# A two-layer hybrid trunk: shifted rows by DMA during the projections, with token shift, convolution and silus computed there

## The chip, the cores and the metric

The kernel runs on one core of one Trainium2 chip. The time is device microseconds of one execution; the number compared is the median of the runs. Engines are named as in the profile: PE (TensorE; PEld is its weight loads), DVE (VectorE), ACT (ScalarE), POOL (GpSimd) and SP (SyncE). Each has its own instruction queue and runs it in order; semaphores order them against each other. DMAs are issued by SP, ACT and POOL.

## The reference

384 tokens (128 context, 256 latent) of width 1024 pass two layers, all in float32. Each layer is a modulated norm, an input projection, a pair of mixers, an output projection, and a mixture of 64 experts. Two steps between projection and mixers mix neighbouring tokens of one sequence. In layer 0 a token shift, on the last 1792 of 2560 columns:

```python
def centred_token_shift(x, mu):
    xp = jnp.pad(x, ((0, 0), (1, 1), (0, 0)))
    neighbours = 0.5 * (xp[:, :-2] + xp[:, 2:])
    return x + mu * (neighbours - x)
```

In layer 1 a convolution over three neighbouring tokens with a weight per column and tap, followed by a silu, on 1536 of 3600 columns; and a silu of 512 further columns (z) that multiplies the delta mixer's normed output at its end:

```python
cqkv = jax.nn.silu(centred_depthwise_conv(cqkv, p['c_conv']))
oc = rms_norm(oc, p['c_onorm']) * jax.nn.silu(heads(cz))
```

The context tokens and the latent tokens are separate sequences, so the rows before the first and after the last token of each count as zero.

## The kernel before

Tokens lie on partitions, 128 to a tile: tile 0 is the context, tiles 1 and 2 the latents. The projection's result `proj` is in SBUF as [128 partitions, 3 tiles, columns]. A neighbouring token is thus on the next partition; between tiles 1 and 2 it is on the far end of another tile.

The work is written out by hand as one program per engine, in phases. `end_phase` makes PE, ACT and DVE wait for each other. In the projection (a loop over column blocks `EVEN_BLOCKS` or `ODD_BLOCKS`, and in each over three tiles; k counts the tiles) PE multiplies into six PSUM banks in turn; DVE copies even k to SBUF, ACT odd k, and PE waits before tile k for the copy of tile k - 6 (the semaphores `proj_saved`). Beside its copies DVE makes the sums for the query and key norms after k = 6 (`head_sums`) and the norms and rotations after k = 8, 10 and 12 (`head_norm`). Weights come into a ring of six slots by SP, which waits only for free slots.

After layer 0's projection `token_shift` (PE L616, DVE L1607) works in four blocks of 448 columns: PE multiplies each tile by a shift matrix of ones beside the diagonal, with an extra matmul for the edge between tiles 1 and 2, and DVE makes three operations per tile. Meanwhile ACT issues `load_cached` (L1214), the loads of cached keys, values, states and small weights: eight DMAs in layer 0, three in layer 1. A second `end_phase` closes the step.

After layer 1's projection `convolution` (PE L631, DVE L1618) works in three blocks of 512 columns: PE makes two shifted copies in six banks, DVE five operations per tile, and PE waits for DVE before the next block. Then ACT (`conv_silu`, L1231) makes exp(-x) of each tile's 1536 columns and DVE adds one, takes the reciprocal and multiplies. `load_cached` comes after the phase's end.

`attend` starts with PE's transposes of queries and keys. ACT first issues two output stores, then copies the transposed queries; the first scores wait for these copies and for the cached keys and values (`parts_loaded`). In `delta`'s last lines ACT makes exp(-z) behind a reciprocal root, and DVE, which waits for both, scales the output, makes the sigmoid of z (`sigmoid_of`, L1504), multiplies it by z and then into `mixed`, for which the output projection waits.

POOL clears corners of the mixers' matrices, loads parameters after each layer's mixers, and runs the experts' gathers and scatters. Most helpers have one line for all their calls: PE's `mm` L544, DVE's tensor_tensor L1485, scalar_tensor_tensor L1493, copy L1499 and reciprocal L1502, ACT's activation L1139.

## Time and profile before

| | |
|---|---|
| median of three runs | 2902.38 us (2894.6 to 2909.49) |
| the profiled execution | 2891.6 us, span 2889.9 us |
| PE busy | 2235.4 us, 77% of the span |
| DVE busy | 871.9 us, 30% |
| ACT busy | 337.0 us, 12% |
| POOL busy | 178.5 us, 6% |
| layer 0's projection (58.5 to 166.6 us) | 108.1 us, PE busy 106.84 |
| token shift, to attention's first transpose | 166.6 to 195.5 us |
| layer 1's projection (1549.7 to 1710.8 us) | 161.1 us, PE busy 158.63 |
| convolution, then silus, to attention's first transpose | 1710.8 to 1767.6 to 1807.0 us |
| silu of z at the delta mixer's end | 2099.8 to 2112.3 us |

Busy shares are averages over stages with different limits; what one stage costs is read from its own stretch and from what ends the waits there. A timeline row gives the start, the duration (of all instructions that it merges), the engine, the line, the operation, its output and inputs, the shapes, the count, and in brackets the engine's idle time before it with what ended it. ACTq, SPq and POOLq are those engines' DMA issues. A row of the table of stretches gives the stretch and its length, the busy time and instructions of PE, PEld, DVE, ACT and POOL, the mean granted clock of PE as a share of 2.4 GHz, the DMA engines' busy share and GB/s.

### The profile page before, as it was taken

The page shows a single profiled execution, that of the slowest core. Times are in us where ns is not written, and L with a number is a line of the kernel's source. Part 1 is how long each engine was busy: PE and PEld are TensorE (multiplying, and loading weights), DVE is VectorE, ACT ScalarE, POOL GpSimd, SP SyncE. Part 2 cuts the span into 40 slices and gives each one's busy share as a digit, 9 for nine tenths or more (in the row PEclk, how much of TensorE's full clock was granted, in tenths as well). Part 3 has the DMA queues.
Part 4 walks back from the last instruction along what each step waited for, and adds up shares of the span by engine and source line. Part 5 has one row for each costly group of instructions (what it writes and reads, how often), then busy time and mean ns, then how long its engine had stood idle before and what let it go on. Part 6 is the DMA issues. An engine that isn't in the chain of part 4 may idle for free.

```text
span 2889.9 us, 37837 instructions
## 1 busy us (share of the span) xinstructions
PE 2235.4 (77%) x16075; PEld 1520.3 (53%) x16075; DVE 871.9 (30%) x1512; ACT 337.0 (12%) x747; POOL 178.5 (6%) x200
## 2 busy tenths in 40 slices
PE   5978887777778888898937981957667788889882
PEld 1445666666645555555513440657665555555551
DVE  1243333333452111111132317265636211111114
ACT  0013111111011111111100000300000111111110
POOL 0000000000001111111100000000000111111110
PEclk9985878877888999999978986568888999999996
DMA  7220323311325999999980220000002799999995
GB/s 282 102 77 15 126 97 119 118 60 60 48 110 215 384 377 381 386 372 372 369 346 29 88 88 0 22 1 3 7 19 97 261 390 391 381 382 382 371 381 197
DMA packets 120703, 571.19 MB, mean 198 GB/s; under 512 B 24944, under 2 KB 28272, under 8 KB 69072
## 3 DMA queue, kind: packets, MB, share of 16 engines
q1 hardware_dynamic: 85392, 496.07, 44.2%
q0 software_dynamic: 28448, 60.42, 6.2%
q10 hardware_dynamic: 6688, 12.18, 1.2%
q8 instruction: 133, 2.18, 0.3%
q14 instruction: 42, 0.34, 0.0%
HBM read 566.42 MB, written 48.30 MB: 213 GB/s over the span
## 4 chain that ended last, share of the span: by engine, by line
PE 61%; DMA 17%; DVE 15%; issue 3%; ACT 1%; SPq 1%; PEldq 0%; PEld 0%; POOL 0%; DVEq 0%; ACTq 0%; POOLq 0%
PE bank L544 56%; DMA ring<-in_exp_w_up 11%; DVE arena L1485 9%; DMA ring<-in_exp_w_down 3%; DMA ring<-in_mod_w 2%; DVE arena L1502 1%; PE bank L1047 1%; PE bank L676 1%; DVE arena L1493 1%; PE bank L1071 1%; DVE mixed L1485 1%; DMA arena<-choice_rows 1%; DVE arena L1499 1%; DVE hT L1490 1%; ACT arena L1139 1%
## 5 line engine op out<-in xcount | busy, mean ns | idle before, releaser
L544 PE MATMUL bank<-ring,arena 128*64 128x256 f32 (+3 forms) x5168 | 928.9, 443 | 137.7 <-DMA ring<-in_exp_w_up 85.8
L544 PEld LDWEIGHTS bank<-ring,arena 128*64 128x64 f32 (+1 forms) x5168 | 570.5, 157 | 463.8 <-issue 357.0
L544 PE MATMUL bank<-arena 64*64 64x64 f32 (+8 forms) x6176 | 426.1, 255 | 54.7 <-DVE arena L1485 41.8
L544 PEld LDWEIGHTS bank<-arena 64*64 64x64 f32 (+5 forms) x6176 | 367.6, 161 | 89.4 <-DVE arena L1485 41.5
L1499 DVE COPY arena<-bank 128x512 f32<-128x512 f32 (+4 forms) x231 | 151.7, 663 | 624.8 <-PE bank L544 560.4
L544 PE MATMUL bank<-ring,hT 128*128 128x512 f32 (+2 forms) x672 | 265.5, 555 | 21.9 <-DVE hT L1490 18.9
L1493 DVE SCALAR_TENSOR_TENSOR arena<-bank,arena 128x256 f32<-128x256 f32 (+2 forms) x96 | 47.5, 494 | 682.3 <-PE bank L544 681.6
L544 PEld LDWEIGHTS bank<-ring,hT 128*128 128x128 f32 x672 | 128.4, 200 | 159.0 <-issue 136.5
L1485 DVE TENSOR_TENSOR arena<-arena 128x512 f32<-128x512 f32 (+9 forms) x175 | 155.1, 909 | 53.8 <-DMA arena<-choice_rows 42.7
L544 PE MATMUL bank<-arena,consts 64*64 64x64 f32 (+5 forms) x516 | 114.7, 417 | 64.2 <-DVEq L1630 20.6
L2173 POOL DMA_INDIRECT arena<-token_rows,arena x80 | 80.6, 1008 | 933.2 <-PE bank L1047 642.7
L544 PE MATMUL bank<-hT,ring 128*128 128x384 f32 x384 | 125.6, 488 | 4.0 <-DVE arena L1485 2.3
L544 PEld LDWEIGHTS bank<-arena,consts 64*64 64x64 f32 (+2 forms) x516 | 59.9, 208 | 109.5 <-issue 62.8
L544 PEld LDWEIGHTS bank<-hT,ring 128*128 128x128 f32 x384 | 104.8, 274 | 23.0 <-DVE arena L1485 3.6
L1047 PE MATMUL bank<-consts,arena 128*128 128x128 f32 x640 | 100.1, 280 | 15.7 <-DMA arena<-token_rows,arena 15.7
L2179 POOL DMA_INDIRECT choice_rows<-arena x80 | 79.7, 996 | 345.0 <-DVE arena L1499 341.1
L1485 DVE TENSOR_TENSOR arena<-bank,consts 128x256 f32<-128x256 f32 (+1 forms) x156 | 74.4, 501 | 84.7 <-PE bank L544 84.7
L1047 PEld LDWEIGHTS bank<-consts,arena 128*128 128x128 f32 x640 | 75.7, 144 | 38.3 <-issue 35.0
L1485 DVE TENSOR_TENSOR arena<-arena,bank 128x512 f32<-128x512 f32 (+3 forms) x150 | 82.5, 563 | 32.9 <-PE bank L544 31.8
L544 PE MATMUL bank<-ring,cond 128*2 128x256 f32 x768 | 61.0, 466 | 32.0 <-DMA ring<-in_mod_w 32.0
L1139 ACT ACTIVATE arena<-bank 128x256 f32<-128x256 f32 (+3 forms) x104 | 42.7, 423 | 352.2 <-PE bank L544 352.2
L1429 ACT COPY arena<-bank 128x256 f32<-128x256 f32 x80 | 29.8, 372 | 451.3 <-PE bank L1071 451.3
(166 smaller groups left out, 1190.8 us busy)
## 6 DMA issues: line engine op xcount, KB each, us to landing
ring<-in_exp_w_gate SPq DMA_DIRECT2D x128, 1024.0 KB, 10.4
ring<-in_exp_w_up SPq DMA_DIRECT2D x128, 1024.0 KB, 10.1
ring<-in_exp_w_down SPq DMA_DIRECT2D x128, 1024.0 KB, 10.3
ring<-in_mod_w SPq DMA_DIRECT2D x48, 1024.0 KB, 9.2
arena<-choice_rows POOLq DMA_DIRECT2D x6, 3072.0 KB, 11.3
ring<-in_od_w_in SPq DMA_DIRECT2D x14, 1024.0 KB, 8.6
ring<-in_ev_w_in SPq DMA_DIRECT2D x10, 1024.0 KB, 15.3
ring<-in_ev_w_out SPq DMA_DIRECT2D x4, 1024.0 KB, 8.8
```

What stands on the lines that cost most here:

```text
L544: return nc.tensor.matmul(out, lhsT, rhs, start=start, stop=stop, **kw)
L676: last = nc.tensor.transpose(bank[2 + u % 2][:, k * P:(k + 1) * P], A.p[:, u % 2, k * P:(k + 1) * P], C["ident"])
L1047: last = nc.tensor.transpose(bank[half][:, c * P:(c + 1) * P], g_x[x.b][:, (4 * half + c) * P:(4 * half + c + 1) * P], C["ident"])
L1071: last = nc.tensor.transpose(bank[4][:, c * P:(c + 1) * P], g_h[x.b][:, c::2], C["ident"])
L1139: return nc.scalar.activation(out, in_, func, **kw)
L1429: nc.scalar.copy(g_ht[x.b], heads(bank[4][:, 0:2 * P], 2)).then_inc(sem("ht_saved"), 1)
L1485: return nc.vector.tensor_tensor(out, a, b, op)
L1490: return nc.vector.tensor_scalar(out, a, s1, s2, op0, op1)
L1493: return nc.vector.scalar_tensor_tensor(out=out, in0=a, scalar=s, in1=b, op0=op0, op1=op1)
L1499: return nc.vector.tensor_copy(out, a)
L2173: nc.gpsimd.indirect_dma_start(g_x[x.b], None, x_rows[l], row(x, 0), bounds_check=NTOK - 1, oob_is_err=False).then_inc(sem("expert_loaded" ...
L2179: nc.gpsimd.indirect_dma_start(y_rows[l], row(x, 1), g_y[x.b], None, bounds_check=TOP_K * NTOK - 1, oob_is_err=False).then_inc(sem("scatte ...
```

## The change

The shift matrices, the shift and convolution steps on PE, and the separate silu steps are gone. While a projection runs, ACT issues for each finished block of shifted columns (four in layer 0, three in layer 1, each of up to 512 columns by three tiles) six SBUF-to-SBUF DMAs that write the block displaced by one partition down (`back`) and up (`ahead`): each displaced copy is made of a block of 112 and one of 15 partitions, and two single rows bridge tiles 1 and 2. POOL clears the edge partitions beforehand. DVE computes shift and convolution from the block and its two displaced copies, two or three tiles later, for all three tiles at once. In layer 1 ACT makes the sigmoids, of the convolved blocks and of z, by exp, ln and exp, and DVE multiplies. Layer 0's last block is loaded and shifted after the last tile. The sigmoids' scratch is `mixed`; the displaced copies lie in the part of the arena that attention uses later, so `load_cached` comes after the phase's end in both layers. The second `end_phase` stays.

The layout, and the steps taken out of PE's order:

```diff
+        near_at = [[(po0, po0 + 1536), (17000, 18536)], [(po1, po1 + 1536), (po1 + 3072, 18700)]]
+        SHIFTED = [EVEN_BLOCKS[2:], ODD_BLOCKS[2:5]]
+        SHIFT_DONE = [3 * (2 + i) + 2 for i in range(4)]
...
-                (token_shift if l % 2 == 0 else convolution)()
```

ACT:

```diff
+            def saved(eng, l, k):
+                eng.wait_ge(sem("proj_saved", 0), 9 * l + k // 2 + 1)
+                eng.wait_ge(sem("proj_saved", 1), 9 * l + (k + 1) // 2)
+
+            def load_near(l, i):
+
+                (a, b), n = SHIFTED[l][i], len(SHIFTED[0]) * l + i
+                saved(act, l, SHIFT_DONE[i])
+                act.wait_ge(sem("near_cleared"), l + 1)
+                if i >= 2:
+                    act.wait_ge(sem("near_used"), n - 1)
+                x = proj_of(l)[0][:, :, a:b]
+                back, ahead = (buf[:, :, 0:b - a] for buf in near[l][i % 2])
+                s = sem("near_loaded", i % 2)
+                for p, q in ((0, P - 16), (P - 16, P - 1)):
+                    load(back[p + 1:q + 1, :, :], x[p:q, :, :], s)
+                    load(ahead[p:q, :, :], x[p + 1:q + 1, :, :], s)
+                load(back[0:1, 2, :], x[P - 1:P, 1, :], s)
+                load(ahead[P - 1:P, 1, :], x[0:1, 2, :], s)
+
+            def sigmoid_block(i):
+
+                if i < 3:
+                    act.wait_ge(sem("near_used"), len(SHIFTED[0]) + i + 1)
+                else:
+                    saved(act, 1, SHIFT_DONE[3])
+                if i >= 2:
+                    act.wait_ge(sem("silu_done"), i - 1)
+                e = wide_scratch[i % 2].rearrange("p (t n) -> p t n", t=TILES)
+                link(f(e, proj1[:, :, 512 * i:512 * (i + 1)], ACT.Exp, scale=-1.0))
+                link(f(e, e, ACT.Ln, bias=one_col))
+                f(e, e, ACT.Exp, scale=-1.0).then_inc(sem("sigmoid_ready"), 1)
...
                     for t in range(TILES):
+                        if l and k in (12, 15, 18, 20):
+                            sigmoid_block((12, 15, 18, 20).index(k))
+                        for i in range(len(SHIFTED[l])):
+                            if k == SHIFT_DONE[i] + 1:
+                                load_near(l, i)
                         if k % 2 == 1:
                             act.wait_ge(sem("proj_ready"), 18 * l + k + 1)
...
+                if l == 0:
+                    load_near(0, 3)
                 end_phase()
...
-                if l % 2:
-                    conv_silu()
-                else:
-                    load_cached(l)
-                end_phase()
-                if l % 2:
-                    load_cached(l)
+                end_phase()
+                load_cached(l)
                 attend(l)
```

DVE:

```diff
+            def shift_block(i):
...
+                dve.wait_ge(sem("near_loaded", i % 2), 96 * (i // 2 + 1))
+                link(tt(tmp, back[:, :, 0:n], ahead[:, :, 0:n], ALU.add))
+                link(stt(tmp, tmp, 0.5, x, ALU.mult, ALU.subtract))
+                link(tt(tmp, tmp, r_mu[:, a - XB:b - XB].unsqueeze(1).broadcast_to([P, TILES, n]), ALU.mult))
+                tt(x, x, tmp, ALU.add).then_inc(sem("near_used"), 1)
...
+            def convolve_block(i):
...
+                dve.wait_ge(sem("near_loaded", i % 2), 96 * (i // 2 + 3))
+                tt(back, back, tap(0), ALU.mult)
+                tt(ahead, ahead, tap(2), ALU.mult)
+                link(tt(x, x, tap(1), ALU.mult))
+                link(tt(x, x, back, ALU.add))
+                tt(x, x, ahead, ALU.add).then_inc(sem("near_used"), 1)
...
+            def gate_block(i):
...
+                dve.wait_ge(sem("sigmoid_ready"), i + 1)
+                tt(x, x, wide_scratch[i % 2].rearrange("p (t n) -> p t n", t=TILES), ALU.mult).then_inc(sem("silu_done"), 1)
...
+                        if l and k in (14, 17, 20, 22):
+                            gate_block((14, 17, 20, 22).index(k))
+                        for i in range(3):
+                            if k == SHIFT_DONE[i] + 3:
+                                (convolve_block if l else shift_block)(i)
                         k += 1
-                end_phase()
+                if l == 0:
+                    shift_block(3)
+                end_phase()
```

The end of `delta`, on ACT and DVE:

```diff
-                f(silu_z, proj1[:, :, CZ:CZ + 512], ACT.Exp, scale=-1.0).then_inc(sem("head_rstd"), 1)
...
-                link(sigmoid_of(silu_z))
-                link(tt(silu_z, silu_z, proj1[:, :, CZ:CZ + 512], ALU.mult))
-                tt(mixed[:, :, 0:512], mixed[:, :, 0:512], silu_z, ALU.mult).then_inc(sem("mixed_ready"), 1)
+                tt(mixed[:, :, 0:512], mixed[:, :, 0:512], proj1[:, :, CZ:CZ + 512], ALU.mult).then_inc(sem("mixed_ready"), 1)
```

POOL:

```diff
+            def clear_near(l):
+
+                for back, ahead in near[l]:
+                    nc.gpsimd.memset(back[0:32, :, :], 0.0)
+                    nc.gpsimd.memset(ahead[96:P, :, :], 0.0)
+                pool.drain().then_inc(sem("near_cleared"), 1)
+
+            clear_near(0)
...
+            for other in MEMBERS:
+                pool.wait_ge(sem("phase_done", other), 8)
+            clear_near(1)
```

## Rows read from the trace of the kernel before

**Rows 1.** The page: shares of the chain of work that ended last, by engine
```profile
PE 61%; DMA 17%; DVE 15%; issue 3%; ACT 1%; SPq 1%; PEldq 0%; PEld 0%; POOL 0%; DVEq 0%; ACTq 0%; POOLq 0%
```

**Rows 2.** Table of stretches: token shift, convolution, silus (columns as told above)
```profile
166.60:195.50 28.90, 15.84 (x41) 7.39 (x41) 22.49 (x36) 0.37 (x1) 0.00 (x0) 0.89 0.36 114
...
1710.80:1767.60 56.80, 25.80 (x48) 10.57 (x48) 29.43 (x45) 0.04 (x1) 0.00 (x0) 0.75 0.10 37
...
1767.60:1807.00 39.40, 0.00 (x0) 0.02 (x1) 37.41 (x9) 4.23 (x3) 0.00 (x0) 0.50 0.00 0
```

**Rows 3.** Timeline of layer 0 from the projection's end to the first scores
```profile
166.62 0.37 ACT L1208 COPY arena<-bank 128x256 f32<-128x256 f32 x1 [6.53 <-PE bank L544]
...
167.16 0.33 ACTq L1151 DMA_DIRECT2D arena<-in_keys_a  x1
...
171.23 0.47 ACTq L1151 DMA_DIRECT2D params<-in_b_g  x1
...
195.49 1.08 PE L652 MATMUL bank<-consts,arena 128*128 128x128 f32 x4 [8.18 <-DVEq L255]
...
196.83 0.58 ACT L1246 COPY arena<-bank 128x512 f32<-128x512 f32 x1 [29.84 <-PE bank L655]
...
199.65 0.68 PE L544 MATMUL bank<-arena 64*128 64x128 f32 x4 [0.72 <-ACT arena L1246]
```

**Rows 4.** Timeline, layer 0's projection, VectorE's copies of even tiles
```profile
113.63 0.69 DVE L1499 COPY arena<-bank 128x512 f32<-128x512 f32 x1 [7.64 <-PE bank L544]
...
155.83 0.69 DVE L1499 COPY arena<-bank 128x512 f32<-128x512 f32 x1 [8.94 <-PE bank L544]
...
163.16 0.43 DVE L1499 COPY arena<-bank 128x256 f32<-128x256 f32 x1 [6.64 <-PE bank L544]
```

**Rows 5.** Groups by form: busy us, mean ns | idle us before
```profile
L1493 DVE SCALAR_TENSOR_TENSOR arena<-bank,arena 128x448 f32<-128x448 f32 x12 | 7.5, 625 | 8.3 <-PE bank L544 7.6
```

**Rows 6.** DMA view: GB/s in 40 slices; issues, KB, us to landing
```profile
GB/s 282 102 77 15 126 97 119 118 60 60 48 110 215 384 377 381 386 372 372 369 346 29 88 88 0 22 1 3 7 19 97 261 390 391 381 382 382 371 381 197
...
token_rows<-arena ACTq DMA_DIRECT2D x2, 1536.0 KB, 5.3
...
ring<-in_sh_w_up SPq DMA_DIRECT2D x2, 1024.0 KB, 9.6
...
params<-in_b_mu ACTq DMA_DIRECT2D x1, 896.0 KB, 28.5
...
arena<-in_values_d ACTq DMA_DIRECT2D x1, 256.0 KB, 4.0
```

**Rows 7.** Timelines of single engines, layer 1, projection to attention
```profile
1615.33 0.69 DVE L1499 COPY arena<-bank 128x512 f32<-128x512 f32 x1 [4.53 <-PE bank L544]
...
1635.14 1.23 DVE L1485 TENSOR_TENSOR arena<-arena 128x1024 f32<-128x1024 f32 x1
...
1657.60 0.69 DVE L1499 COPY arena<-bank 128x512 f32<-128x512 f32 x1 [6.93 <-PE bank L544]
...
1687.51 22.71 PE L544 MATMUL bank<-ring,hT 128*128 128x512 f32 x48 [0.26 <-issue]
...
1710.26 0.58 ACT L1208 COPY arena<-bank 128x512 f32<-128x512 f32 x1 [13.15 <-PE bank L544]
...
1807.01 1.09 PE L652 MATMUL bank<-consts,arena 128*128 128x128 f32 x4 [49.73 <-DVEq L255]
```

**Rows 8.** Timeline, end of layer 1's delta mixer
```profile
2094.67 1.47 ACT L1139 ACTIVATE arena<-arena 128x1536 f32<-128x1536 f32 x1
...
2096.17 1.76 DVE L1485 TENSOR_TENSOR mixed<-mixed,stats 128x1536 f32<-128x1536 f32 x1 [1.99 <-ACT arena L1139]
...
2099.76 0.96 DVE L1489 TENSOR_SCALAR arena<-arena 128x1536 f32<-128x1536 f32 x1
...
2112.33 1.76 DVE L1485 TENSOR_TENSOR mixed<-mixed,arena 128x1536 f32<-128x1536 f32 x1
```

**Rows 9.** Table of stretches: a part of layer 1's attention
```profile
1835.00:1882.00 47.00, 47.00 (x147) 31.39 (x146) 11.18 (x27) 13.65 (x40) 0.00 (x0) 0.50 0.00 1
```

More of the change, by code:

```diff
@@ L402, in build @@
         conv_w = params[:, 0:4608].rearrange("p (k n) -> p k n", k=3)
-        conv_exp = lambda t: arena[:, po1 + 1536 * t:po1 + 1536 * (t + 1)]
-        conv_tmp = arena[:, po1 + 4608:po1 + 5632]
-        silu_z = arena[:, po1 + 1536:po1 + 3072].rearrange("p (t n) -> p t n", t=TILES)
+        near_at = [[(po0, po0 + 1536), (17000, 18536)], [(po1, po1 + 1536), (po1 + 3072, 18700)]]
+        near = [[[arena[:, a:a + 1536].rearrange("p (t n) -> p t n", t=TILES) for a in pair] for pair in sets]
+                for sets in near_at]
+        wide_scratch = [mixed[:, :, :].rearrange("p t n -> p (t n)")[:, 1536 * i:1536 * (i + 1)] for i in range(2)]
+        SHIFTED = [EVEN_BLOCKS[2:], ODD_BLOCKS[2:5]]
+        SHIFT_DONE = [3 * (2 + i) + 2 for i in range(4)]
         mod_rows = [arena[:, a:a + 256] for a in (16384, 16640)]
@@ L1229, in load_cached @@
                     load(r_g2, w["b_g2"][0], s)
-            def conv_silu():
-                for t in range(TILES):
-                    act.wait_ge(sem("conv_done"), t + 1)
-                    f(conv_exp(t), proj1[:, t, 0:1536], ACT.Exp, scale=-1.0).then_inc(sem("conv_exp_ready"), 1)
             def attend(l):
@@ L1355, in delta @@
                 act.wait_ge(sem("head_sumsq"), 5)
-                rsqrt(stats[:, 12:24], 1.0 / P, eps6)
-                f(silu_z, proj1[:, :, CZ:CZ + 512], ACT.Exp, scale=-1.0).then_inc(sem("head_rstd"), 1)
+                rsqrt(stats[:, 12:24], 1.0 / P, eps6).then_inc(sem("head_rstd"), 1)
                 act.wait_ge(sem("stored"), 96)
@@ L1589, in head_norm @@
                 dve.wait_ge(sem("qk_ready"), TILES * l + t + 1)
+            def shift_block(i):
+                (a, b), (back, ahead) = SHIFTED[0][i], near[0][i % 2]
+                n = b - a
+                x = proj0[:, :, a:b]
+                tmp = wide_scratch[0][:, 0:TILES * n].rearrange("p (t n) -> p t n", t=TILES)
+                dve.wait_ge(sem("near_loaded", i % 2), 96 * (i // 2 + 1))
[3 more added lines that the diff above has]
+                tt(x, x, tmp, ALU.add).then_inc(sem("near_used"), 1)
+                dve.wait_ge(sem("near_used"), i + 1)
+            def convolve_block(i):
+                (a, b), (back, ahead) = SHIFTED[1][i], near[1][i % 2]
+                x = proj1[:, :, a:b]
+                tap = lambda k: conv_w[:, k, a:b].unsqueeze(1).broadcast_to([P, TILES, b - a])
+                dve.wait_ge(sem("near_loaded", i % 2), 96 * (i // 2 + 3))
[4 more added lines that the diff above has]
+                tt(x, x, ahead, ALU.add).then_inc(sem("near_used"), 1)
+                dve.wait_ge(sem("near_used"), len(SHIFTED[0]) + i + 1)
+            def gate_block(i):
+                x = proj1[:, :, 512 * i:512 * (i + 1)]
+                dve.wait_ge(sem("sigmoid_ready"), i + 1)
+                tt(x, x, wide_scratch[i % 2].rearrange("p (t n) -> p t n", t=TILES), ALU.mult).then_inc(sem("silu_done"), 1)
             def projection(l):
-                proj, _ = proj_of(l)
                 k = 0
@@ L2133, in _ @@
                 projection(l)
-                (token_shift if l % 2 == 0 else convolution)()
                 end_phase()
```

56 lines of the change are left out of this document (removed).

## The prediction

> **What bounds the kernel now.** I read the page's chain of waits first: most of the span is PE work and expert DMA, with DVE at 15% [rows 1]. Shares of the whole say little about a change in three places, so I next read the table of stretches around them [rows 2]. In the token shift (28.9 us) PE is busy 15.84 and DVE 22.49. In the convolution (56.8 us) it is 25.80 and 29.43: the two take turns, since block b+1 waits for banks that DVE empties. In the stretch of the silus (39.4 us) PE does nothing and DVE 37.41. No other work is put there; all three stand between the last projection tile and attention, so each of their microseconds is on the path. The timelines then give the ends: layer 0's projection closes with ACT's copy at 166.62 and attention's first transpose is at 195.49 [rows 3]; in layer 1 it is 1710.26 and 1807.01 [rows 7]. At the end of the delta mixer DVE makes a silu of z alone, from 2096 to 2114 [rows 8]. Inside the projections, by contrast, DVE has gaps: between two copies it is free from 156.5 to 163.16 [rows 4].
>
> **Layer 0.** Removed: 40 matmuls and 36 DVE operations, all between 167 and 195.3. Added: per block of 512 columns six ACT-issued copies and four DVE operations of 1536 elements a partition. A tensor_tensor of that size took 1.76 us [rows 8]; the scalar form has no row at that size, but at 448 elements it took 0.625 [rows 5], and 0.625 to 1.76 over 1088 elements is 1.04 ns each, which is also tensor_tensor's slope elsewhere, so I take 1.76. With 0.03 of gap a block is 4 x 1.79 = 7.2 us. The last block has 768 elements: 0.625 + 320 x 1.04 ns = 0.96, so 4 x 0.99 = 3.95.
>
> Placing them in DVE's order: block 0 stands after the second head norm, with most of two tiles ahead of it. Block 1 stands after the copy at 155.83 [rows 4] and runs 156.5 to 163.7, which delays the copy of 163.16 by 0.5; no tile waits for that one. Block 2 runs 164.2 to 171.4. Block 3 needs its own copies, issued by ACT after the copy that ends at 167.0. ACT issued eight DMAs from 167.16 to 171.70, 0.57 each [rows 3], so six take 3.4 us.
>
> Landing: no row moves SBUF to SBUF. A full block is 2 x 127 x 3 x 2 KB = 1.56 MB; the nearest row by size and queue is the token rows, 1536 KB in 5.3 us from issue, the nearest busy one 9.6 for 1 MB beside another load [rows 6]. I take 6.5 us from the first issue for a full block, and 5.5 for the half-wide last one (3.4 of issue, 2 of tail): 172.6. Ends: 171.4, where block 2 hides it all, and 176.7 by the 9.6. Block 3 then ends at 176.5, and with two phase ends PE starts near 176.9 instead of 195.49.
>
> Not all of this arrives. load_cached stood in ACT's queue beside the token shift, which hid it; now its eight issues (4.5 us) stand after the phase end, with the two output stores and the copies of the transposed queries queued behind them, and the first scores wait for those. Before, the first copy came 1.34 us after the first transpose [rows 3]. Now it is 176.9 + 4.5 + 0.9 = 182.3, three copies end at 184.0, and the scores start at 184.1 instead of 199.65. **Gain 15.5 us**, ends 11.4 and 16.7.
>
> **Layer 1.** Removed: 48 matmuls, 45 DVE operations and the silus with three reciprocals, all of 1710.8 to 1807. Added on DVE: per block five tensor_tensors of 1.76 (8.95 us with gaps) and per gate one (1.8). Added on ACT: per sigmoid three activations of 1536, 1.47 each [rows 8], 4.6 us with gaps, for four blocks.
>
> The order is a chain between DVE, ACT and DMA. DVE convolves block 0 from 1636.4, where the head norm ends [rows 7], to 1645.4. ACT, which waits in its sigmoid for exactly this, ends at 1650.0, and only then issues block 1's copies: landed at 1656.5. DVE copies at 1657.60 [rows 7], gates (1660.1) and convolves block 1 to 1669.0. ACT: sigmoid to 1673.6, copies of block 2 landed by 1680.1. DVE: convolution to 1689.1, ACT: sigmoid of block 2 to 1693.7, of z to 1698.3. The last gate stands after the last even tile's copy and ends near 1706, before ACT's last copy ends at 1710.84 [rows 7]. So all of it is covered by projection matmuls, with 5 us of slack at the end.
>
> What the added waits hold up: odd tiles, whose copies stand behind them in ACT's queue. The worst is the one copied right behind block 2's DMAs, at 1677.5; its bank is wanted again by the block that starts at 1687.51 [rows 7], six tiles on, so PE isn't held, with 10 us to spare. The clearing on POOL goes ahead of the delta corners and waits for the end of layer 0's experts; POOL is idle there and the first copies come half a projection later, so I cost it at nothing; without that cover block 0 would wait, which has 14 us before DVE wants it.
>
> PE's first transpose moves from 1807.01 to some 1711.2: 95.8 us. Against that, the cached values took 4.0 us alone [rows 6] and the first scores wait for them; now they are issued 1 us after SP's two shared-expert loads, of which one landed in 9.6 [rows 6]. Ends 0 and 5.6, I take 2.5, nearer the lone row since the two queues share the engines. **Gain 93.3 us.**
>
> **End of the delta mixer.** Gone are z's exponential (1.47) that DVE waited for to 2096.17, and add, reciprocal and product from 2099.76 to 2112.33, 12.57 [rows 8]. The last product stays. **Gain 13.9 us**; nothing else was late there.
>
> **Sum.** 15.5 + 93.3 + 13.9 = 122.7 us. The profiled execution took 2891.6 (span 2889.9), so it would take 2769. It is faster than all three timed runs, whose median 2902.38 I compare with: **2780 us**.
>
> On the copies a rule of the Trainium skill bears ("DMA: Bandwidth & Descriptors", section "Why a DMA increments its semaphore by 16 and not by 1"): a DMA is split over the largest number of engines up to 16 that divides its slowest dimension, so 112 rows go over 16, 15 over 15 and 127 over a single one. No run here shows a copy of such heights. By that rule the blocks spread as I assume, and the single engine of the rival below isn't met.
>
> **The rivals.** (a) *The copies run on one engine.* In the expert stage 16 engines move about 382 GB/s [rows 6], 24 each; 1.56 MB would need 65 us. Layer 0's 3.5 blocks in a row from 114 [rows 4] would end at 342 and attention start 169 us after my 177; layer 1's chain (from the copy at 1615.33 [rows 7]: 1616 + 3 x 65 + 48 of convolutions, sigmoids and gates) ends at 1859 instead of 1711. In all 6.5 us per us of a block's time, less 106: +317, so 3097, **slower**. It decides the sign above 35 us a block. For it: no row shows such a shape. Against: every row over many partitions is far quicker. (b) *Late landing.* The worst row is 28.5 us, in a queue filled at the start [rows 6]. Then layer 0 loses 23 and layer 1 1616 + 85.5 + 48 - 1711 = 39: 2842. Against it: during the projections DMA is mostly idle. (c) *Attention at full clock.* Layer 1's attention would follow dense matmuls at once instead of an idle PE. Before, that attention had a granted clock of 0.50 (1.2 GHz) with PE busy 47.00 of 47.00 us [rows 9]. At 2.4 GHz it could give back at most half, 24 us: 2756. Against: PE filled that stretch at 0.50 and wasn't raised. The Trainium skill ("TensorE: Matmul & The Clock Gate", section "Part 1: The HAM clock gate (the "warmup" mystery)") says that sustained activity releases the throttle; by that rule (c) would hold, and this row is against it.
>
> **How the numbers follow.** Forecast 2780: 0.85; (a) 0.03; (b) 0.05; (c) 0.07. The forecast's terms move it by 4.1 + 3.1 up and 1.2 + 2.5 down; with the runs' own spread of 2894.6 to 2909.49 (7 each way) it lies within 2769 to 2794. A stall in ACT's new order, which the slack of 5 and 10 us doesn't cover, would put it some 18 further (a block's landing, its convolution and a gate: 6.5 + 8.95 + 1.8), so I close at 2812; below, (c) with a few us of spread takes it to 2750. 0.5% (14 us) is about what a measurement here can tell from no change: faster 0.96, same 0.01, slower 0.03, from (a).
>
> **What would show it.** Right: attention's first transposes come some 0.5 us after layer 1's last projection copy and some 10 after layer 0's, no long reciprocal is left, PE's last projection block stays at 22.71 us [rows 7], and the first scores of layer 0 wait for ACT. Wrong: DVE idle in the projections before a copy of shifted rows lands, or ACT's last copies later than PE's last tile.

## The result

The changed kernel took 2769.58 us (median; 2753.74 to 2775.42) beside 2899.4 us (2894.6 to 2909.49) of the kernel before: a ratio of 0.9539 with a 95% interval of 0.9491 to 0.9588. Measured again later it was 2772.17 us beside 2898.74, and 0.955 (0.9522 to 0.9578). The forecast was 2780, 2750 to 2812. The total came out near the forecast, but one of its three terms did not, as the trace shows.

The profiled execution of after took 2767.51 us (span 2765.9), that of before 2891.6 (span 2889.9). The page of after, shares of the chain of work that ended last (compare [rows 1]):

```profile
PE 62%; DMA 19%; DVE 12%; issue 4%; ACT 1%; SPq 1%; PEldq 1%; PEld 0%; ACTq 0%; POOL 0%; DVEq 0%; POOLq 0%
```

DVE's share fell from 15 to 12%, which is most of what was removed; shares don't say where. The timeline of layer 0 of after does, from DVE's last copies to the first scores. It answers [rows 3, 4]:

```profile
157.70 4.78 ACTq L1123 DMA_DIRECT2D arena<-arena  x6
...
164.75 0.42 DVE L1500 COPY arena<-bank 128x256 f32<-128x256 f32 x1
174.96 1.76 DVE L1486 TENSOR_TENSOR mixed<-arena 128x1536 f32<-128x1536 f32 x1 [9.79 <-DMA arena<-arena]
...
185.10 0.96 DVE L1486 TENSOR_TENSOR arena<-arena,mixed 128x768 f32<-128x768 f32 x1
...
186.48 1.08 PE L625 MATMUL bank<-consts,arena 128*128 128x128 f32 x4 [18.72 <-DVEq L255]
...
190.77 0.90 ACTq L1123 DMA_DIRECT2D out_k_a<-arena  x1
191.71 0.85 ACTq L1123 DMA_DIRECT2D out_v_a<-arena  x1
...
194.26 1.19 PE L547 MATMUL bank<-arena 64*128 64x128 f32 x4 [4.34 <-ACT arena L1253]
```

Block 2's six copies were issued from 157.70 on, and DVE waited 9.79 us for them: they landed 17.3 us after the first issue, not 6.5. From there all is late: the transposes at 186.48, and the scores at 194.26 instead of 199.65 before. The copies' landing beside what ran with them, by the DMA view of after over 150 to 200 us and, below, over 1655 to 1672 us of layer 1 (KB each, median us from issue to landing):

```profile
ring<-in_mod_w SPq DMA_DIRECT2D x3, 1024.0 KB, 8.1
arena<-arena ACTq DMA_DIRECT2D x2, 672.0 KB, 12.0
...
arena<-arena ACTq DMA_DIRECT2D x2, 90.0 KB, 12.5
```

```profile
ring<-in_od_w_out SPq DMA_DIRECT2D x2, 1024.0 KB, 5.7
arena<-arena ACTq DMA_DIRECT2D x2, 672.0 KB, 5.8
arena<-arena ACTq DMA_DIRECT2D x2, 90.0 KB, 5.6
```

The same copies took 12 us in layer 0 and 5.8 in layer 1. In layer 0 SP's modulation weights are released by the same end of a PE block as the copies; that suggests contention, and an experiment has to say.

Layer 1 of after, single engines from the first convolution to the first scores (answers [rows 7]):

```profile
1624.41 5.09 DVE L1486 TENSOR_TENSOR arena<-arena,params 128x1536 f32<-128x1536 f32 x3
...
1647.88 5.09 DVE L1486 TENSOR_TENSOR arena<-arena,params 128x1536 f32<-128x1536 f32 x3
...
1666.78 1.07 ACT L1218 COPY arena<-bank 128x512 f32<-128x512 f32 x2 [5.58 <-PE bank L547]
...
1668.90 5.10 DVE L1486 TENSOR_TENSOR arena<-arena,params 128x1536 f32<-128x1536 f32 x3 [5.92 <-DMA arena<-arena]
...
1672.84 23.80 PE L547 MATMUL bank<-ring,hT 128*128 128x512 f32 x48 [0.26 <-issue]
...
1690.42 1.75 DVE L1486 TENSOR_TENSOR arena<-arena,mixed 128x1536 f32<-128x1536 f32 x1
...
1696.68 0.59 ACT L1218 COPY arena<-bank 128x512 f32<-128x512 f32 x1 [9.42 <-PE bank L547]
...
1697.56 0.63 PE L625 MATMUL bank<-consts,arena 128*128 128x128 f32 x4 [0.91 <-ACTq L255]
...
1706.22 0.80 PE L547 MATMUL bank<-arena 64*128 64x128 f32 x4 [5.85 <-DMA arena<-in_values_d]
```

The last gate (from 1690.42) ends 5 us before ACT's last copy (from 1696.68) does, and the transposes follow that copy at once: what took from 1710.8 to 1807 before now lies beside projection matmuls. The scores then wait for the cached values.

**A ledger of stretches.** The landmarks are ACT's, in the profiled executions of before and after: the end of its last projection copy, the reading of the sums of its first softmax, its first copy in the output projection, the start of the next norm.

| Stretch, us | before | after | gain |
|---|---|---|---|
| start to layer 0's last projection copy | 166.99 | 168.17 | -1.2 |
| to its first softmax | 33.75 | 27.48 | 6.3 |
| to its output projection and router's norm | 596.11 | 597.88 | -1.8 |
| router and experts 0 | 732.46 | 725.23 | 7.2 |
| to layer 1's last projection copy | 181.53 | 178.51 | 3.0 |
| to its first softmax | 102.76 | 10.36 | 92.4 |
| its attention's softmaxes | 65.98 | 66.20 | -0.2 |
| to its output projection | 235.86 | 217.13 | 18.7 |
| router's norm, router and experts 1 | 774.46 | 774.94 | -0.5 |

The span's 124.0 us are the sum. The change's own places give 6.3 + 92.4 and, of the 18.7, the 13.9 of z's silu: 112.6. The other 11.4 stand in stretches whose code is the same.

### The profile page after: what moved, and what is told of

Read it like the earlier page. It is cut to its first block, busy times and chain, and to the rows that moved or that the text cites. A ratio compares the mean times of both kernels' runs of the same rounds, so it can differ in the third digit from the quotient of the medians.

```text
span 2765.9 us, 37670 instructions
## 1 busy us (share of the span) xinstructions
PE 2183.0 (79%) x15987; PEld 1491.0 (54%) x15987; DVE 828.7 (30%) x1454; ACT 349.5 (13%) x755; POOL 190.0 (7%) x208
## 4 chain that ended last, share of the span: by engine, by line
PE 62%; DMA 19%; DVE 12%; issue 4%; ACT 1%; SPq 1%; PEldq 1%; PEld 0%; ACTq 0%; POOL 0%; DVEq 0%; POOLq 0%
PE bank L547 57%; DMA ring<-in_exp_w_up 12%; DVE arena L1486 7%; DMA ring<-in_exp_w_down 3%; DMA ring<-in_mod_w 2%; PE bank L1020 1%; PE bank L649 1%; DVE mixed L1486 1%; PE bank L1044 1%; DMA arena<-choice_rows 1%; DVE hT L1491 1%; DVE arena L1500 1%; PE bank L742 1%; DVE arena L1494 1%; ACT arena L1111 1%
## 5 line engine op out<-in xcount | busy, mean ns | idle before, releaser
L1494 DVE SCALAR_TENSOR_TENSOR arena<-bank,arena 128x256 f32<-128x256 f32 (+1 forms) x84 | 40.0, 476 | 670.4 <-PE bank L547 670.2
L1486 DVE TENSOR_TENSOR arena<-arena 128x1024 f32<-128x1024 f32 (+7 forms) x147 | 138.6, 970 | 52.6 <-DMA arena<-choice_rows 42.3
L1020 PE MATMUL bank<-consts,arena 128*128 128x128 f32 x640 | 100.1, 280 | 15.9 <-DMA arena<-token_rows,arena 15.9
L547 PE MATMUL bank<-arena,consts 64*64 64x64 f32 (+4 forms) x428 | 72.8, 372 | 38.3 <-ACT arena L1111 16.5
L1082 PE MATMUL bank<-consts,arena 128*128 128x128 f32 x48 | 9.8, 393 | 90.7 <-DVEq L2122 90.7
```

Source lines behind the costliest of these rows:

```text
L547: return nc.tensor.matmul(out, lhsT, rhs, start=start, stop=stop, **kw)
L1020: last = nc.tensor.transpose(bank[half][:, c * P:(c + 1) * P], g_x[x.b][:, (4 * half + c) * P:(4 * half + c + 1) * P], C["ident"])
L1486: return nc.vector.tensor_tensor(out, a, b, op)
L1494: return nc.vector.scalar_tensor_tensor(out=out, in0=a, scalar=s, in1=b, op0=op0, op1=op1)
```

## Experiments

The runs are named e1 to e11 and a2. Kernels of one job were timed together with the kernel before, and ratios are to that; e1 to e4 are one job, a2 and e5 to e7 another, e8 to e10 a third, e11 a fourth.

**The two layers apart (e1, e2).** First layer 0's shift by DMA alone, with layer 1 as before (in the loops of ACT and DVE; PE's convolution and the silus come back):

```diff
-                        if l and k in (12, 15, 18, 20):
-                            sigmoid_block((12, 15, 18, 20).index(k))
-                        for i in range(len(SHIFTED[l])):
+                        for i in range(0 if l else len(SHIFTED[l])):
...
+                if l:
+                    convolution()
```

> Layer 0's token shift by DMA as in the changed kernel; layer 1's convolution, its silus and z's silu as in the kernel before. Theory A (read from the two traces): the change gave layer 0 only 5.4 us at attention's first scores (199.65 to 194.26), since block 2's copies landed 17.3 us after their first issue and load_cached came out from its cover; the rest of the 124 us comes from layer 1 (92), z (14) and some 11 us of the experts' stage that vary from execution to execution. So 5 to 7 us below the kernel before, ratio 0.998. Theory B (the prediction's step): layer 0 gives 15.5 us, or it carries the experts' 11 us with it: ratio 0.9945 or lower.

Measured: 2884.04 us beside 2892.39 in the same job, ratio 0.9963 (0.9946 to 0.9979), 11 us less (6 to 16). The first softmax came 27.60 us after the last projection copy (33.75 before, 27.48 in after): 6.2 us, as theory A has it. The time alone doesn't decide: A's 0.998 and B's 0.9945 lie just outside either end of the interval. The experts of layer 0 took 728.87 us; they don't follow the shift.

Then layer 1's part alone, with PE's token shift back in layer 0:

```diff
-                        for i in range(len(SHIFTED[l])):
+                        for i in range(len(SHIFTED[1]) if l else 0):
...
+                if l == 0:
+                    token_shift()
```

> Token shift of layer 0 as in the kernel before; convolution, silus and z's silu of layer 1 as in the changed kernel. Theory A: 92.4 + 13.9 = 106 us below the kernel before, ratio 0.963, and in the profile the first scores of layer 1 come about 10 us after ACT's last projection copy. Theory B: if the experts' 11 us belong to layer 1's edits (POOL's clearing or the earlier loads), 117 us, ratio 0.9596.

Measured: 2793.17 us, ratio 0.9644 (0.9612 to 0.9676), 103 us less (94 to 112); 10.33 us from the last copy to the first softmax. Theory A's 106 holds, and B's 117 lies outside. By the ratios the two parts add up to 114 us.

**z's silu put back to the end of the delta mixer (e3).**

```diff
-                rsqrt(stats[:, 12:24], 1.0 / P, eps6).then_inc(sem("head_rstd"), 1)
+                rsqrt(stats[:, 12:24], 1.0 / P, eps6)
+                f(silu_z, proj1[:, :, CZ:CZ + 512], ACT.Exp, scale=-1.0).then_inc(sem("head_rstd"), 1)
...
+                link(sigmoid_of(silu_z))
+                link(tt(silu_z, silu_z, proj1[:, :, CZ:CZ + 512], ALU.mult))
```

> The changed kernel with z's silu put back to the end of the delta mixer (the exponential, the add, reciprocal and product there); all else as changed. The prediction's step: 13.9 us above the changed kernel, some 2783, with the add, reciprocal and product back between the reduction and the output projection's transposes. Rival: z's sigmoid and gate cost something inside the projection (they stand in ACT's and DVE's queues there), so that taking them out gives some back: less than 10 us above.

Measured: 2793.49 us, ratio 0.9652 (0.962 to 0.9684), 24 us above the changed kernel's 2769.58 of another job; the intervals of the two ratios allow 13.9. What the other 10 us are isn't shown. The timeline of DVE at the end of its delta mixer shows what came back:

```profile
1994.37 1.76 DVE L1488 TENSOR_TENSOR mixed<-mixed,params 128x1536 f32<-128x1536 f32 x1
1996.16 0.96 DVE L1492 TENSOR_SCALAR arena<-arena 128x1536 f32<-128x1536 f32 x1
1997.16 9.75 DVE L1505 RECIPROCAL arena<-arena 128x1536 f32<-128x1536 f32 x1
2006.95 1.76 DVE L1488 TENSOR_TENSOR arena<-arena 128x1536 f32<-128x1536 f32 x1
2008.74 1.76 DVE L1488 TENSOR_TENSOR mixed<-mixed,arena 128x1536 f32<-128x1536 f32 x1
```

From 1996.16 to 2008.74 are 12.58 us, the prediction's 12.57; in after the product stands right behind the product with the parameters. The first softmax of layer 1 came 9.86 us after the last copy, against 10.36: z's sigmoid and gate cost at most 0.5 us there, and the rival falls.

**Why block 2 landed late: the weights held (e4).**

```diff
                 wait_slot_free(sp, n)
+                if n == mods_at[0, 2] + 3:
+                    sp.wait_ge(sem("near_loaded", 0), 192)
+                    sp.wait_ge(sem("near_loaded", 1), 192)
```

> SP holds the modulation weights from the fourth piece on until blocks 2 and 3 of layer 0 have landed; all else as changed. Theory A (the copies share the DMA engines with the weights that PE's same tile boundary releases): block 2 lands 7 to 9 us after its first issue instead of 17.3, DVE doesn't wait for it (runs 166.7 to 173.9), block 3 lands near 177.5, attention's first transposes come near 182 and the first scores near 190 instead of 194.26: some 4.3 us less. The held pieces are wanted at 275, so nothing else moves. Theory B (the copies are slow by their own shape: 15 partitions, single rows, 2 KB pieces): landing stays at 15 us or more and scores at 194. Theory C (ACT's issue alone sets it, 4.8 us for six): landing stays some 5 us after the sixth issue either way.

The timelines of this kernel, and its DMA view over 150 to 185 us:

```profile
155.99 6.71 ACTq L1126 DMA_DIRECT2D arena<-arena  x6
...
165.36 1.76 DVE L1489 TENSOR_TENSOR mixed<-arena 128x1536 f32<-128x1536 f32 x1 [1.91 <-DMA arena<-arena]
...
177.04 1.09 PE L628 MATMUL bank<-consts,arena 128*128 128x128 f32 x4 [11.03 <-DVEq L255]
...
185.53 1.22 PE L550 MATMUL bank<-arena 64*128 64x128 f32 x4 [5.05 <-DMA arena<-in_values_a]
```

```profile
arena<-arena ACTq DMA_DIRECT2D x2, 672.0 KB, 5.9
...
arena<-arena ACTq DMA_DIRECT2D x2, 90.0 KB, 5.7
...
arena<-in_values_a ACTq DMA_DIRECT2D x1, 64.0 KB, 8.2
```

Nothing of the copies changed, and they landed in 5.9 us instead of 12.0, the 15-partition ones in 5.7 instead of 12.5: block 2 came 9.4 us after its first issue instead of 17.3. Contention it is; the copies' shape isn't slow. Issuing is the larger part of what is left, 6.71 us for six. The first softmax came 20.5 us after the last copy, 7.0 less than in after where theory A had 4.3, but with 8.2 us for the cached values: the released weights now met those. In time it can't be told from the changed kernel, 2768.98 us and 0.9556 (0.9502 to 0.961).

**The exposed loads of layer 0 (e5).** Beside the held weights, the cached keys and values are loaded at the projection's start, and the other loads and stores go through SP:

```diff
-        near_at = [[(po0, po0 + 1536), (17000, 18536)], ...
+        near_at = [[(po0, 13664), (17000, 18536)], ...
...
+                    sp.wait_ge(sem("near_loaded", 1), 192)
+                    load_state()
...
+                if l == 0:
+                    load(attention[0].klat[:, :, 0, :], w["keys_a"].unsqueeze(1), sem("parts_loaded"))
+                    load(attention[0].vc, w["values_a"], sem("parts_loaded"))
```

> As e4 (weights held), and beside that layer 0's cached keys and values are loaded at the start of the projection (one buffer of shifted rows moves to a free place for that), and its six state loads and two stores are issued by SP ahead of the held weights instead of by ACT between the transposes and the query copies. Theory A: the exposed load_cached was the rest of the lost gain: in e4 ACT issued for 5.6 us ahead of its query copies and PE then waited for the cached values until 185.5; without both the first softmax comes 16.2 us after the last projection copy (27.5 in the changed kernel, 20.5 in e4, 33.75 in the kernel before): 11 us under the changed kernel, near the prediction's 15.5 us gain in layer 0 plus what its block 2 lost. Theory B: the query copies or DVE's copies of the keys are the next bound at once, and no more than 1 us is gained over e4.

Measured: 2759.96 us, ratio 0.9524 (0.9493 to 0.9554), 12 us by the medians under the changed kernel in the same job, whose interval overlaps. The first softmax came 16.05 us after the last copy (16.2 expected), and between the transposes and the scores PE's timeline shows no wait left but ACT's copies:

```profile
177.46 1.09 PE L642 MATMUL bank<-consts,arena 128*128 128x128 f32 x4 [10.91 <-DVEq L255]
...
181.62 1.19 PE L564 MATMUL bank<-arena 64*128 64x128 f32 x4 [0.72 <-ACT arena L1264]
```

Of the 33.75 us of before 17.7 are gone now, so the prediction's 15.5 were there to be had. Of the 9.2 us that after fell short of them, holding the weights alone gave back 7.0 (e4); that is the contention. The rest of what e5 gained are the loads and stores behind the phase end, which the prediction had counted as a cost, at 4.5 + 0.9 us.

**The changed kernel once more (a2)**, unedited, on the 11.4 us that no place of the change owns.

> The changed kernel itself once more. By the landmarks of five executions the three places give 6.2 + 92.4 + 13.9 = 112.5 us, but its first comparison had 0.9539, 134 us. Theory A: the three places are all; what is beyond 112 is how the experts' weights and the stretch after layer 0's attention happen to run, so the ratio comes out nearer 0.96 and the stretches of the three places repeat (27.5 and 10.4 us from the last projection copy to the first softmax, 217 to 222 us of delta). Theory B: the change gives some 20 us more in a place that I haven't found; the ratio stays at 0.954 or lower.

Measured: 0.955 (0.9522 to 0.9578). The three places repeated (28.02, 10.06 and 219.71 us), and the other stretches vary with the execution: over the kernels run here experts 0 took 725 to 735 us, layer 1's projection 177.2 to 182.1 where nothing delays it, the stretch to layer 1's output projection 217.1 to 222.7 where z's silu isn't in it. But the ratio stayed where it was, 127 to 130 us by the medians, so A's 0.96 fell. The profiled execution of before lay 8 us under its own median; where those 8 us lie, and why the whole comes out some 15 us beyond its two parts measured apart, stays open. A part of it is in e2's profiled execution, whose stretch from layer 0's first softmax to its output projection took 560 us, 549 in before and 550 in after, with the same code.

**Layer 1's cached keys and values early (e6)** (the values straight to their place, the keys copied from a free part of the constants):

```diff
-        near_at = ..., [(po1, po1 + 1536), (po1 + 3072, 18700)]]
+        near_at = ..., [(po1, po1 + 1536), (14896, 18700)]]
...
+                if l:
+                    load(early_keys, w["keys_d"], sem("parts_loaded"))
+                    load(attention[1].vc, w["values_d"], sem("parts_loaded"))
```

> As the changed kernel, but layer 1's cached keys and values are loaded at the start of its projection (the keys to a free part of the constants, copied by ACT during the transposes; one buffer of shifted rows moved to free the values' place). PE then goes from the projection to the scores with under 3 us of pause. Theory A: the scores come 3.5 us earlier (10.4 to 6.9 us from the last projection copy) and the attention still runs at a granted clock of 0.50, its 66 us unchanged. Theory B (rival c of the prediction, with the pause for the cached values as what drops the clock): without the pause the attention keeps the 1.0 of the projection, and its 66 us become some 42.

Measured: 2769.46 us, ratio 0.9554 (0.9526 to 0.9583). The profiled execution is the one of six that stands apart: 2741.28 us at a granted clock of 0.866 over the whole execution, the others 2766.78 to 2778.29 at 0.855 to 0.864. In it the attention ran at full clock. Tables of stretches over the attention's softmaxes, first the changed kernel run again, then this one:

```profile
1713.00:1779.00 66.00, 65.69 (x194) 42.18 (x195) 18.14 (x47) 20.38 (x69) 0.00 (x0) 0.50 0.01 5
```

```profile
1707.00:1745.00 38.00, 36.76 (x197) 24.39 (x197) 18.59 (x49) 20.29 (x69) 0.00 (x0) 1.00 0.14 47
```

The same work in 38.0 us at 1.0 (2.4 GHz) instead of 66 at 0.50 (1.2 GHz). So neither theory holds alone: without the long pause the attention may keep the clock that the projection left, and by the times of the other five mostly doesn't. The loads themselves gave 5.0 us (10.06 to 5.05), where A had 3.5.

**All three together (e7)**, the sum of these edits.

```diff
-        near_at = [[(po0, po0 + 1536), (17000, 18536)], [(po1, po1 + 1536), (po1 + 3072, 18700)]]
+        near_at = [[(po0, 13664), (17000, 18536)], [(po1, po1 + 1536), (14896, 18700)]]
```

> The changed kernel with the weights held and the cached keys and values of both layers early (e4, e5 and e6 together). Theory A: the gains add, 11.3 + 3.5 = 15 us under the changed kernel, ratio to the kernel before 0.955 or lower. Theory B: what layer 0 gains is given back in the stretch behind it, which waits for modulation weights: less than 8 us.

Measured: 2758.99 us, ratio 0.9473 (0.9429 to 0.9517). Four of six executions took 2758.66 to 2761.99, two 2736.22 and 2725.47; their granted clocks were 0.857 to 0.865 in the four and 0.868 and 0.879 in the two. By the landmarks 28.02 became 16.11 and 10.06 became 5.06: 17 us, so the gains add. In the profiled execution, of 2761.99 us, the clock fell early in the attention:

```profile
1694.00:1698.00 4.00, 4.00 (x18) 2.88 (x18) 0.88 (x3) 2.36 (x12) 0.00 (x0) 0.80 0.99 323
1698.00:1758.00 60.00, 60.00 (x177) 38.06 (x177) 17.27 (x44) 17.52 (x55) 0.00 (x0) 0.50 0.01 2
```

**The pauses of PE filled (e10)**, by idle matmuls into a bank that the attention doesn't use:

```diff
+            def fill(l):
+                for _ in range(2 * l):
+                    mm(bank[6][:, :], C["ident"], consts[:, 0:512])
...
                     pe.drain().then_inc(sem("ring_released"), 1)
+                fill(l)
                 end_phase()
...
                     last.then_inc(sem("qkT_ready"), 1)
+                fill(l)
...
+                    if u == 1:
+                        fill(l)
```

> As e7 (all three), with two idle matmuls of 512 columns on PE in each of the three pauses of layer 1 between the last projection tile, the transposes, the scores and the first turned probabilities (0.9 us each), and nothing else. In e6's profile the attention kept a granted clock of 1.0 and took 38.0 us, in e7's it fell to 0.50 some 4 us into it and took 64.7. Theory A: the short pauses ahead decide; filled, the attention keeps 1.0 in most executions, so at least half of the times lie under 2740 and the median is 2737 or lower. Theory B: the pauses don't decide it; times as in e7, a median of 2755 to 2762 with one or two lower ones.

Measured: 2738.19 us, ratio 0.9459 (0.9427 to 0.9491); all six executions between 2720.82 and 2741.97, five of them under 2740. The median is 1.2 us above the bound that A set; by the spread A holds and B's 2755 falls. The profiled execution is the fastest, 2720.82 us. Its table of stretches, first three pauses and scores, then the attention:

```profile
1675.00:1690.00 15.00, 14.44 (x65) 8.11 (x63) 3.44 (x8) 5.79 (x19) 0.00 (x0) 1.00 0.60 210
1690.00:1700.00 10.00, 9.56 (x48) 6.13 (x48) 6.09 (x17) 5.15 (x20) 0.00 (x0) 1.00 0.01 2
1700.00:1710.00 10.00, 10.00 (x56) 6.67 (x57) 4.28 (x10) 5.47 (x18) 0.00 (x0) 1.00 0.00 0
```

The attention took 38.83 us. The granted clocks of the six were 0.866 to 0.878, all above the four long executions of e7. So the pauses of some 0.9 us each, in which PE waited for DVE and ACT, bear on whether the attention keeps the clock. They don't decide it alone: e6's profiled execution had the same pauses and kept it. And by their ratios to before, in two jobs, e7 and e10 can't be told apart (0.9429 to 0.9517 and 0.9427 to 0.9491); what differs is that four of six executions lie near 2760 us in e7 and none in e10.

**The same in layer 0 (e11)**, with one idle matmul a pause and eleven in the 10.85 us before the transposes:

```diff
-                fill(l)
+                fill(1 if l else 11)
                 end_phase()
```

> As e10, but each idle matmul of 512 columns took 0.94 us there, so two of them outlast a pause of 0.9; now one stands in each of layer 1's three pauses. Layer 0 gets the same, and eleven in the 10.85 us in which PE stands between its projection and the transposes, while the last shifted blocks are finished. In e10 PE's granted clock fell from 1.0 to 0.50 in that pause, and layer 0's attention ran at 0.50 for 64 us, as in every kernel so far. Theory A: what holds for layer 1 holds for layer 0; its attention keeps 1.0 and takes some 38 us, 26 less, layer 1's scores come 2.4 us earlier than in e10 and its attention stays near 39: a median near 2711. Theory B: layer 0's attention, with products of 64 columns, isn't enough to keep the clock, which falls some us into it: 2735 to 2740.

Measured: 2723.18 us, ratio 0.9389 (0.9363 to 0.9414), the fastest kernel here; five of six executions took 2715.3 to 2728.06, and the ratio is theirs; the sixth took 2759.21. The median lies between A's 2711 and B's 2735. Its profiled execution, of 2728.06 us, goes with B for layer 0:

```profile
166.00:176.00 10.00, 9.89 (x25) 4.48 (x24) 9.71 (x7) 0.37 (x1) 0.00 (x0) 1.00 0.43 114
176.00:180.00 4.00, 3.07 (x19) 1.89 (x17) 1.97 (x5) 1.59 (x3) 0.00 (x0) 1.00 0.93 243
180.00:186.00 6.00, 5.94 (x30) 3.99 (x29) 1.68 (x6) 3.36 (x18) 0.00 (x0) 1.00 1.01 373
186.00:192.00 6.00, 6.00 (x17) 3.34 (x16) 1.14 (x3) 2.22 (x11) 0.00 (x0) 0.52 0.75 304
```

But for 0.93 us ahead of the transposes, at 177 us, PE was busy all through, and the clock still fell at some 186 us, in layer 0's attention, whose softmaxes took 61.5 us instead of 64. Layer 1's took 38.00, with its scores 1.6 us earlier than in e10. By the landmarks that is 6.7 us in all; the median moved 15, between two jobs. What else moved isn't shown.

**Rival (a), one copy of 127 partitions (e8).**

```diff
-                for p, q in ((0, P - 16), (P - 16, P - 1)):
+                for p, q in ((0, P - 1),):
```

> The changed kernel with each shifted block copied by one DMA of 127 partitions instead of two of 112 and 15 (four DMAs a block instead of six). Theory A (rival a of the prediction, the rule that the rows are split over the largest number of engines up to 16 that divides them): all of a 127-row copy goes through one engine, some 65 us by the expert stage's 24 GB/s an engine, and the time is near 3097; DVE waits in both projections for the landings, and the copies' landing rows show 30 us or more. Theory B: the rows are spread whatever their number; landing stays at 10 to 12 us, the time within 1% of 2770, and the block of 15 was not needed.

Measured once: 3120.91 us; A had 3097. DVE's timeline, and the table of stretches while a block was under way:

```profile
265.86 1.76 DVE L1486 TENSOR_TENSOR mixed<-arena 128x1536 f32<-128x1536 f32 x1 [54.41 <-DMA arena<-arena]
...
328.68 1.76 DVE L1486 TENSOR_TENSOR mixed<-arena 128x1536 f32<-128x1536 f32 x1 [55.24 <-DMA arena<-arena]
```

```profile
230.00:290.00 60.00, 0.00 (x0) 0.00 (x0) 7.45 (x5) 0.58 (x1) 0.00 (x0) 0.50 0.07 25
```

A DMA share of 0.07 is 1.1 of 16 engines, at 25 GB/s; blocks came 62.8 us apart (65 forecast). The first softmax of layer 0 was 182 us later than in after and layer 1's projection 163 us longer. The split into 112 and 15 is what makes the change a gain.

**The slack of layer 1 (e9)**, with ACT kept busy ahead of each block of copies:

```diff
+                if l:
+                    for _ in range(9):
+                        link(f(arena[:, 15408:16432].rearrange("p (t n) -> p t n", t=2), x[:, 0:2, :], ACT.Square))
```

> The changed kernel, with nine activations of 1024 elements, some 9.5 us, put on ACT ahead of each of layer 1's three blocks of copies (their results go nowhere). It measures the slack that the prediction claimed: 5 us at the last gate, 10 us before a late ACT copy holds PE. Theory A: block 1's copies slip 9.5 us and block 2's some 19; ACT's copy of the tile behind block 2's DMAs comes near 1686 instead of 1667 on the changed kernel's clock, and PE, which wants its bank at 1673.5, stands for some 12 us before the last block; the projection ends 11 to 13 us later, the rest is unchanged. Theory B: the chain has more slack than that (less than 5 us later).

Measured once: 2809.03 us. PE's and DVE's timelines:

```profile
1673.22 5.09 DVE L1489 TENSOR_TENSOR arena<-arena,params 128x1536 f32<-128x1536 f32 x3 [13.41 <-DMA arena<-arena]
...
1703.91 22.73 PE L547 MATMUL bank<-ring,hT 128*128 128x512 f32 x48 [19.49 <-ACT arena L1221]
```

PE stood before the last block for ACT's copy, as A said, but for 19.5 us instead of 12. Block 1's copies, issued from 1659.26 on, met SP's weights there and landed after 14 us, where block 2's in after took 9: the late copies lost their free stretch too. Layer 1's projection took 196.73 us, 15 to 20 above the kernels without the delay, and the time rose by 37 to 39; beside the projection, both experts' stages were among the longest seen (734 us each). So the bound is where the prediction put it, at ACT's copies. Counted from the start of layer 1's norm, the copy behind block 2's DMAs came 24.6 us later than in after and PE's last block 19.3: some 5 us were slack, half of the 10 that the prediction had.

## Why the prediction was right, and where not

*What bounds it.* Right: all that was removed stood on the path. With one layer's part taken out again (e1, e2), or z's (e3), that part of the time comes back.

*Layer 0, 15.5 us: wrong.* By the ledger it was 6.3. The step that failed is the landing of block 2, 6.5 us from the first issue with an upper end of 9.6; it took 17.3. I had said in rival (b) that DMA is mostly idle in the projections, and had not looked at what the end of the same PE block releases on SP: two modulation weights of 1 MB. e4 shows the contention (12.0 to 5.9 us for a copy). A second term was mis-sized: ACT issued six copies in 4.56 to 6.88 us (0.76 to 1.15 each), not 3.4. The 0.57 was read from loads [rows 3]. The exposed load_cached came as written: first softmax held by ACT's queue, 4.4 us of issue, though the two stores took 1.8 instead of 0.9. DVE's share was right: 1.76 and 0.96 us an operation, 7.2 and 3.9 a block. The gain lies outside the ends of 11.4 and 16.7 that I gave this term. A sign that I had named as showing me wrong was there too, DVE idle before a block lands: 9.79 us. In layer 1 it was idle 5.92 us before block 2, but there my own schedule had it wait, from 1669.0 to 1680.1.

*Layer 1, 93.3 us: right, 92.4.* After's projection began 11.5 us earlier than before's (1538.27 instead of 1549.77), so its times stand beside the prediction's less 11.5: conv0 1624.9 (measured 1624.41), conv1 1648.6 (1647.88), block 2 landed 1668.6 (1668.90), last gate ended 1694.5 (1692.17). The 5 us of slack at the last gate hold, and so do the free banks: PE's last block took 23.80 us beside 22.71 [rows 7], with no wait for ACT. But the copy behind block 2's DMAs began 6 us ahead of that block (1666.78 and 1672.84), not 10. The cached values cost 3.5 instead of 2.5.

*End of the delta mixer, 13.9: right* by e3's rows.

*Sum.* 6.3 + 92.4 + 13.9 = 112.6 instead of 122.7. The measured 127 to 130 is more than that, so the total is nearer the forecast than its terms are; part of that is luck, and some 15 us of it are not placed.

*Rivals.* (a) was priced right, 3097 against 3120.91 where it was made to happen in a single run; the rule that I cited for the spread over engines (the Trainium skill, "DMA: Bandwidth & Descriptors", section "Why a DMA increments its semaphore by 16 and not by 1") agrees with the 0.07 of e8. (b) named the right risk for layer 0 at a too high price and a too low chance. (c), given 0.07, did not happen in the profiled execution of after, as the table of stretches shows over most of its attention:

```profile
1707.00:1760.00 53.00, 52.13 (x156) 33.59 (x155) 14.90 (x40) 17.04 (x59) 0.00 (x0) 0.50 0.03 10
```

But it was no impossibility. One of after's other three executions stands apart, 2753.74 us at a granted clock of 0.868 beside 2767.51 to 2775.42 at 0.858 to 0.860; it wasn't profiled, so that its attention kept the clock isn't shown. In the profiled executions of e6, with the wait for the cached values gone, and of e10, with the pauses filled, the attention took 38.0 and 38.8 us instead of 66. That is up to 28 us less, where I had 24 at most, since I halved a window of 47 us [rows 9] and not the whole attention. My argument against it, a busy PE that wasn't raised at 0.50 [rows 9], only showed that it isn't raised from there; it said nothing of one that arrives at 1.0. In before, too, the first scores ran at 1.00 (1812 to 1814 us) and the clock was 0.50 from 1816 us on.

## What to carry to other kernels

Before costing a transfer that moves into a busy stage, list what the same event releases on the other queues: it will share the engines, and here it doubled the landing. Work moved beside matmuls is free only up to the copy that frees a PSUM bank; measure that slack. A stage of small matmuls that follows a dense one is worth joining to it without a pause, since the clock it arrives with may be the one it keeps (layer 1's attention here), or may not (layer 0's).

## What the runs showed of the hardware

- The same attention ran at a granted clock of 1.0 in 38.0 us and at 0.50 in 66 us. At 0.50 PE was busy 60.00 of 60.00 us and was not raised (e7); 1.0 held to the end of layer 1's attention in the profiled executions of e6, e10 and e11, and not of layer 0's in e11. The Trainium skill ("TensorE: Matmul & The Clock Gate", section "Part 1: The HAM clock gate (the "warmup" mystery)") has sustained activity release the throttle; e7's row differs.
- In after a DMA from ACT whose two sides are SBUF took 0.76 to 1.15 us of ACT's queue, where the loads issued there behind the two projections took 0.35 to 0.76.
- Copies of 127 partitions moved at 25 GB/s (e8), of 112 and 15 together at 236 to 318 while they ran alone (the DMA view of after, 1661 to 1666 us).
- Over the profiled executions here the stretch from layer 0's first softmax to its output projection took 543 to 560 us; it was 543 to 546 in all kernels with held weights, and in e8, and 549 and more in the others. Why is open.
